# RWKV stage of a two-block layer kernel: the elementwise part of the next head group moved beside the inverse, and output products moved between steps of the last scan

## The reference

```python
r, k, v, wl, al, gl = jnp.split(feat, splits, axis=-1)
w = -jax.nn.softplus(-(w0 + jnp.tanh(wl) @ w2)) - 0.5
a = jax.nn.sigmoid(a0 + al @ a2)
g = jax.nn.sigmoid(gl) @ g2
kk = heads(k * k_k)
kk = kk * lax.rsqrt(jnp.sum(kk * kk, axis=-1, keepdims=True) + 1e-12)
k = k * (1.0 + (a - 1.0) * k_a)
...
def step(state, inp):
    r_t, k_t, v_t, kk_t, b_t, d_t = inp
    sa = jnp.einsum('bhvk,bhk->bhv', state, -kk_t)
    state = (state * d_t[:, :, None, :] + sa[..., None] * b_t[:, :, None, :]
             + v_t[..., None] * k_t[:, :, None, :])
    return state, jnp.einsum('bhvk,bhk->bhv', state, r_t)
...
x = x + jnp.concatenate([mla_out, rw_out], axis=-1) @ w_o
x = x + hier_moe(rms_norm(x, g_ffn), ...)
```

## Time and profile before

| | us |
|---|---|
| median of 3 runs (2466.19 to 2469.96) | 2467.66 |
| the profiled execution's own time | 2463.41 |
| its span in the trace | 2461.6 |
| RWKV stage, first product of `rows` 0 to `rw_out` 4 | 263.1 to 531.6 |
| output products and router | 531.6 to 566 |

### The profile page before, as it was taken

How to read it: one execution, slowest core, us unless ns; L and a number is a source line. 1 busy time by engine, 2 the same in 40 slices (tenths; PEclk the granted TensorE clock), 3 DMA queues, 4 the chain that set the end, 5 groups by cost and what they waited for, 6 DMA issues and landing times.

```text
span 2461.6 us, 30787 instructions
## 1 busy us (share of the span) xinstructions
PE 2324.6 (94%) x12524; PEld 1654.6 (67%) x12524; DVE 1233.2 (50%) x2169; ACT 746.1 (30%) x1172; POOL 646.4 (26%) x288
## 2 busy tenths in 40 slices
PE   8989787797999989999999999999999999999999
PEld 3334455544444467668878888888766887888887
DVE  4455555533556531774355767310187445577610
ACT  3333222212111143443233333223354223333311
POOL 0000000002000033224444444444313444444443
PEclk9999888878999999999999999999999999999999
DMA  5521000035999932113333333222211333333322
GB/s 220 135 71 35 15 2 2 2 134 196 373 409 409 356 114 88 60 52 95 94 94 95 98 99 94 93 96 98 86 52 61 94 95 93 96 101 94 95 80 99
DMA packets 80258, 287.79 MB, mean 117 GB/s; under 512 B 9299, under 2 KB 10323, under 8 KB 79478
## 3 DMA queue, kind: packets, MB, share of 16 engines
q1 hardware_dynamic: 76726, 279.56, 33.1%
q0 software_dynamic: 1408, 4.20, 0.5%
q10 hardware_dynamic: 1984, 2.06, 0.2%
HBM read 278.11 MB, written 16.07 MB: 120 GB/s over the span
## 4 chain that ended last, share of the span: by engine, by line
PE 80%; DVE 9%; DMA 5%; issue 3%; ACT 2%; POOL 1%; ACTq 0%; SPq 0%; DVEq 0%; another core or an unknown queue 0%; POOLq 0%
PE bank L1899 12%; PE bank L1901 12%; PE bank L1900 12%; PE bank L529 5%; DMA arena<-in_stream 4%; PE bank L2048 3%; PE bank L2049 3%; PE bank L2047 3%; DVE arena L392 3%; PE bank L1513 2%; PE bank L855 2%; PE bank L1884 2%; PE bank L1886 2%; PE bank L1885 2%; PE bank L1481 2%
## 5 line engine op out<-in xcount | busy, mean ns | idle before, releaser
L1634 POOL TENSOR_TENSOR ring_low<-ring,W_high 128x1024 fp32r<-128x1024 f32 x252 | 606.2, 2406 | 1124.5 <-ACT W_high L402 1124.5
L1899 PE MATMUL bank<-H_high,W_high 128*128 128x512 f32 x1408 | 555.5, 395 | 7.9 <-ACT arena L402 5.9
L1901 PE MATMUL bank<-H_high,ring_low 128*128 128x512 f32 x1408 | 548.5, 390 | 0.0
L1900 PE MATMUL bank<-H_low,W_high 128*128 128x512 f32 x1408 | 548.1, 389 | 0.0
L402 ACT ACTIVATE W_high<-ring 128x1024 fp32r<-128x1024 f32 x264 | 279.8, 1060 | 872.2 <-PE bank L1901 552.6
L1899 PEld LDWEIGHTS bank<-H_high,W_high 128*128 128x128 f32 x1408 | 264.3, 188 | 77.9 <-issue 23.2
L1901 PEld LDWEIGHTS bank<-H_high,ring_low 128*128 128x128 f32 x1408 | 264.3, 188 | 55.9
L1900 PEld LDWEIGHTS bank<-H_low,W_high 128*128 128x128 f32 x1408 | 264.4, 188 | 55.7 <-issue 1.9
L392 DVE TENSOR_TENSOR arena<-bank,root 128x512 f32<-128x512 f32 x116 | 79.7, 688 | 309.9 <-PE bank L1901 309.7
L402 ACT ACTIVATE arena<-bank 128x512 f32<-128x512 f32 (+5 forms) x175 | 74.6, 438 | 315.2 <-PE bank L830 115.9
L398 DVE SCALAR_TENSOR_TENSOR arena<-arena 128x512 f32<-128x512 f32 (+3 forms) x63 | 117.8, 1870 | 99.1 <-ACT arena L406 98.5
(11 more groups left out here) (264 smaller groups left out, 3239.2 us busy)
## 6 DMA issues: line engine op xcount, KB each, us to landing
ring<-in_stream SPq DMA_DIRECT2D x289, 512.0 KB, 3.6
arena<-in_stream SPq DMA_DIRECT2D x31, 2048.0 KB, 12.9
arena<-in_stream SPq DMA_DIRECT2D x31, 1024.0 KB, 10.2
sorted_x<-in_zero_row SPq DMA_DIRECT2D x4, 2048.0 KB
arena<-sorted_x SPq DMA_DIRECT2D x15, 512.0 KB, 16.3
X<-in_x SPq DMA_DIRECT2D x2, 1024.0 KB, 7.9
ring<-in_stream SPq DMA_DIRECT2D x1, 2048.0 KB, 7.9
out<-X SPq DMA_DIRECT2D x8, 256.0 KB, 7.0
```

The costliest lines, as they stand in the source:

```text
L1634: return G.tensor_tensor(ring_low[:, slot, :], ring[:, slot, :], W_high[:, s % 2, :].bitcast(F32), ALU.subtract)
L1899: mm(ps[:, :], wh[:, k, :], H_high[:, k, :], start=k == 0, stop=False)
L1900: mm(ps[:, :], wh[:, k, :], H_low[:, k, :], start=False, stop=False)
L1901: i = mm(ps[:, :], wl[:, k, :], H_high[:, k, :], start=False, stop=k == KD - 1)
```

## The change

It has three parts.

1. `rwkv_prepare` is split into `rwkv_early` (`feed`, `rows`, `roots`, `root`, `bonus`, `turned`: the elementwise part, with `rows` and `root` each cut so that the products stand ahead of VectorE's part) and `rwkv_invert` (from `blocks` on). In round c = 0 to 3 the inverse of group c stands beside the scan of group c - 1 and the early part of group c + 1. The products `rg` and the turned `v` move to the end, in `turned`.
2. MT, TT, TKA, XX and MK move to the place of the attention's weights `uq`, which are no longer needed. DVE's wait for `rta` goes. The lower halves m are placed by `HALVES_AT`: three in the opening, then 3 and 4 in round 0, 5 in round 1, 6 and 7 in round 2.
3. For column tiles 0 to 6, contraction tile 4 of the upper half stands between `step` n and `state` n of the last scan, and tiles 5 and 6 behind `state` n, into a bank of their own (`wq{n}`), which DVE adds to X. After the scan only tile 7 is left for them; m = 7 keeps all four.

```diff
+def rwkv_invert(c):
+
+    yield "blocks", c, 0
+    yield "keyed", c, 0
     for lev in LEVELS:
         yield "cross", c, lev
         yield "grow", c, lev
...
-BESIDE = "pss" * 4 + "ps" * 10 + "pspp"
+def rwkv_early(c):
+
+    for part in ("feed", "rows", "roots", "root", "bonus", "turned"):
+        yield part, c, 0
+
+
+EARLY_OUT = 7
+HALVES_AT = {("feed", 0): [0], ("roots", 0): [1], ("bonus", 0): [2], ("feed", 1): [3], ("bonus", 1): [4], ("bonus", 2): [5], ("feed", 3): [6], ("bonus", 3): [7]}
+BESIDE = "iss" * 4 + "e" + "iss" + "e" + "iss" * 2 + "e" + "iss" + "is" + "e" + "is" * 2 + "e" + "ii" + "e"
...
+    for part in rwkv_early(0):
+        yield from with_halves(part)
+    for c in range(4):
+        invert, scan, early = rwkv_invert(c), rwkv_scan(c - 1) if c else iter(()), rwkv_early(c + 1) if c < 3 else iter(())
         for who in BESIDE:
...
+    for part, c, n in rwkv_scan(3):
+        yield part, c, n
+        if part in ("step", "state") and n < EARLY_OUT:
+            yield f"out_{part}", c, n
...
-        W.update(YB=W["LW"], MT=W["LW"], TT=W["A"], TKA=W["KK"], KH=W["KK"], KT=W["KP"], BT=W["B"], XX=W["SQ"], MK=W["RS"],
+        W.update(YB=W["LW"], KH=W["KK"], KT=W["KP"], BT=W["B"],
                  BH=W["ENL"], AT=W["ELX"])
+        for i, n in enumerate(("MT", "TT", "TKA", "XX", "MK")):
+            W[n] = par(w1, W1, "uq", 512 * i, 512)
...
-                for k in range(4, KD):
+                first = KD - 1 if m < EARLY_OUT else 4
+                for k in range(first, KD):
...
+            if part == "half":
+                latent_half(pe, n, range(4))
+            elif part == "out_step":
+                pe.e.wait_ge(*pe.emptied(f"wq{n}"))
+                pe.e.wait_ge(*pe.nth("rw_out", 3))
+                mm(bank_of(f"wq{n}")[:, :], out_weights(pe, n)[:, 4, :], H[:, 4, :], start=True, stop=False)
+            elif part == "out_state":
+                w = out_weights(pe, n)
+                mm(bank_of(f"wq{n}")[:, :], w[:, 5, :], H[:, 5, :], start=False, stop=False)
+                mm(bank_of(f"wq{n}")[:, :], w[:, 6, :], H[:, 6, :], start=False, stop=True).then_inc(pe.fills(f"wq{n}"), 1)
...
-            if part == "rows":
-                if c:
-                    dv.e.wait_ge(*dv.filled(f"rta{c - 1}_1"))
+            if part == "half":
+                add_latent_half(dv, n)
+            elif part == "out_state":
+                dv.e.wait_ge(*dv.filled(f"wq{n}"))
+                if n == 0:
+                    dv.e.wait_ge(*dv.taken("wp7"))
+                tt(X[:, n, :], X[:, n, :], bank_of(f"wq{n}")[:, :], ALU.add).then_inc(dv.takes(f"wq{n}"), 1)
```

More of the change, by code:

```diff
@@ L710, in rwkv_pe @@
             e, q = pe.e, c % 2
-            if part == "rows":
+            if part == "half":
[8 more added lines that the diff above has]
+                mm(bank_of(f"wq{n}")[:, :], w[:, 6, :], H[:, 6, :], start=False, stop=True).then_inc(pe.fills(f"wq{n}"), 1)
+            elif part == "feed":
                 pe.e.wait_ge(*pe.emptied(f"ru{c}"))
@@ L719, in rwkv_pe @@
                 mm(bank_of(f"ra{c}")[:, :], w2a2[64:128, cw], RAW[64:128, 12, 1:513], start=True, stop=True).then_inc(pe.fills(f"ra{c}"), 1)
+            elif part == "roots":
+                pe.e.wait_ge(*pe.emptied(f"rkk{c}"))
+                pe.e.wait_ge(*pe.nth("kksq", c + 1))
+                mm(bank_of(f"rkk{c}")[:, :], cc("blk64"), W["SQ"], start=True, stop=True).then_inc(pe.fills(f"rkk{c}"), 1)
+            elif part == "bonus":
+                pe.e.wait_ge(*pe.emptied(f"rb{c}"))
+                pe.e.wait_ge(*pe.nth("rkr", c + 1))
+                mm(bank_of(f"rb{c}")[:, :], cc("blk64"), W["YB"], start=True, stop=True).then_inc(pe.fills(f"rb{c}"), 1)
+            elif part == "turned":
+                pe.e.wait_ge(*pe.nth("hats", c + 1))
+                for x, src in (("b", W["BH"]), ("k", W["KH"]), ("a", W["AT"]), ("v", RAW[:, 8 + c, 1:513])):
+                    turn_feature(pe, c, x, src)
                 pe.e.wait_ge(*pe.emptied(f"rg{c}"))
@@ L723, in rwkv_pe @@
                 mm(bank_of(f"rg{c}")[:, :], par(w1, W1, "g2", c * P, P), RAW[:, 13, 1:513], start=True, stop=True).then_inc(pe.fills(f"rg{c}"), 1)
[L724 to L739, removed]
             elif part == "blocks":
@@ L986, in rwkv_act @@
             q = c % 2
-            if part == "rows":
+            if part == "feed":
                 if c == 0:
@@ L996, in rwkv_act @@
                 act_(W["A"], bank_of(f"ra{c}")[:, :], ACT.Tanh, bias=small[:, 12 + c:13 + c], scale=0.5).then_inc(sc.takes(f"ra{c}"), 1)
[L997 to L1001, removed]
-                act_(W[f"TKV{q}"], bank_of(f"rt{c}_v")[:, :], ACT.Copy).then_inc(sc.takes(f"rt{c}_v"), 1)
-            elif part == "root":
+            elif part == "roots":
                 log_exp_tables()
@@ L1014, in rwkv_act @@
             elif part == "turned":
-                for x, d in (("b", f"TKB{q}"), ("k", f"TKK{q}"), ("a", "TKA")):
+                for x, d in (("b", f"TKB{q}"), ("k", f"TKK{q}"), ("a", "TKA"), ("v", f"TKV{q}")):
                     sc.e.wait_ge(*sc.filled(f"rt{c}_{x}"))
                     act_(W[d], bank_of(f"rt{c}_{x}")[:, :], ACT.Copy).then_inc(sc.takes(f"rt{c}_{x}"), 1)
+                sc.e.wait_ge(*sc.filled(f"rg{c}"))
+                if c >= 2:
+                    sc.e.wait_ge(*sc.nth("rw_out", c - 1))
+                act_(W[f"G{q}"], bank_of(f"rg{c}")[:, :], ACT.Copy).then_inc(sc.takes(f"rg{c}"), 1)
             elif part == "keyed":
```

31 lines of the change are left out of this document (15 added, 16 removed).

## The result

The change made the kernel a little slower: 2472.6 us (median of 17 runs, 2467.5 to 2473.9) against 2465.9 (17 runs on the same chip), a ratio of 1.0021 with an interval of 1.0015 to 1.0028. I had forecast 2459 and given slower 0.15; it lies just inside my range of 2446 to 2473, on the wrong side of the kernel before. The profiled execution took 2472.6 us, its span is 2470.8, 9.2 more than before.

The account below looks back on a forecast made before the run. Rounds were taken as PE-DVE chains with no engine full. Opening and rounds gain 6.7 us, scan and output 1.8: -8.5 on the profiled 2463.4 gives 2454.9, plus 4.3 to the median: 2459, range 2446 to 2473.

Parts of the forecast that it names:

- the clock term: Rounds 0 to 2: half clock behind each `rows` and `root` wait, 5 us counted, 2.1 on the path, 11 in all.
- my 233.4: Opening and all rounds up to the last scan: 222.4 at full clock plus 11 of clock, against 240.1 before.
- The bricks: Stage and step lengths read from the earlier trace, such as 30.8 us for a round's inverse half, added up for the new order.
- The stalls: PE waiting for DVE's `rows` and `root` in rounds 0 to 2: 3.4 and 4.3 us each.
- The first pass: Round 0, inverse 0 beside early part 1 and lower halves 3 and 4: 46 us before the clock's cost.
- The second step in a level: A second scan step between `cross` and `grow` of an inverse level shows as 2.4 us, at best 0.3.
- The last scan: Three output products join each step; PE bounds it at 4.2 us instead of 2.4: 12.6 more, plus 1.6 of clock.
- rival 3: The last scan stays at half clock, a step takes 7.5 us, the kernel is slower at 2482; chance 0.14.
- The output: Column tiles 1 to 6 lose three products each, 16.2 us, less 2.3 for a half-clock start: 13.9 saved.
- tile 7's weights: Output stage: they land at 13.9 us after `rw_out` 4, PE needs them at 14.6, fitting by little.
- 1 (full clock): The clock stays full in the rounds: -23.4 us in all, 2444; chance 0.15.
- Rival 2: Each `rows` and `root` delays the chain by its whole length, 1.4 us more six times: 2467.5, no change; chance 0.23.

Follow-up runs that it names:

- part 3 alone: The kernel before with only the output products placed between the steps of the last scan, rounds untouched: 2469.15 us, ratio 1.0012.
- the shifted order: The changed kernel with `state` n - 1 right ahead of `step` n instead of right behind `step` n - 1: 2468.51 us, ratio 1.0012.
- the shifted order with the halves in the stalls: The changed kernel with `state` n - 1 right ahead of `step` n and lower output halves moved over `rows` and `root`: 2453.54 us, ratio 0.9946.

## Why the prediction was wrong

- **The step that failed** is the clock term: "Six times, and nearly always: 11 us", for "two stalls of 3.4 and 4.3 us in each of rounds 0 to 2". There are three pauses in rounds 1 and 2 and one in round 3, since DVE's masks of `blocks` hold PE up for 1.7 and 1.1 us. And the third costs 5.3 us by the rows from `keyed` to `feed`, where I had 1.8 for each. Covering it with idle products took 13.8 us off the kernel and made the three rounds 14.6 us shorter in all; the opening and the rounds came out 13.3 above my 233.4. The kernel before waits in `blocks` too, but once and not twice, and its clock held there in rounds 1 and 2; I took the 30.8 us of that half of the round as a brick, and the clock that was in it with it.
- **The length of a stretch at half clock** was mis-sized too. I counted 5 us behind each stall, and had read the earlier trace rows as one pause with its half clock up to 336. The trace before has two, a wait of 3.42 us up to 318.0 and one of 4.86 up to 327.8, with full clock between them:

```profile
320.00:322.00 2.00, 2.00 (x4) 0.81 (x3) 0.58 (x1) 1.95 (x5) 0.00 (x0) 0.50 0.00 0
323.00:325.00 2.00, 0.00 (x0) 0.00 (x0) 1.97 (x4) 0.00 (x0) 0.00 (x0) 1.00 0.00 0
```

Behind the first the clock was at half for 3 us, behind the second for 10. In the changed kernel it was 6 and 3 us behind the two stalls of round 0, and 10 and 7 in rounds 1 and 2: 43 in all where I had 30.
- **The bricks added up, in part by luck.** Where that pause is covered by idle products and nothing else is changed, rounds 1 to 3 take 60.1, 62.9 and 39.5 us. I had 56 and 59.6, with 3.7 of clock on each, and 41: 59.7, 63.3 and 41. But the second step was too dear (below), and it hid that the stalls' half clock lasted 17 and 13 us in these two rounds and not 10. That this kernel ran at 2458.8 us, where I had forecast 2459 for the changed one, is luck as well: its stages are 0.8 us shorter than my 292.2 (300.7 less 8.5), the parts ahead of and behind them 4.1 us longer than before, and the 4.3 that I had added from the profiled execution to the median are 2.5 by the 17 runs.
- **The stalls** of `rows` and `root` are 3.25 and 3.82 us in round 0, and 4.0 and 3.7 in rounds 1 and 2, forecast 3.4 and 4.3, with DVE as releaser and half clock behind each.
- **The first pass** took 49.2 us, forecast 46 and 3.7 of clock.
- **The second step in a level** I took at 2.4 us. That is the step of the earlier trace rows, which runs at half clock, in a sum that was to hold at full clock. In round 3 of the changed kernel, at full clock and with no elementwise part beside it, the levels with two steps follow each other every 5.90 us (L854 begins a `state`; the other one of the level stands between these two, at 488.02), against 4.34 with one:

```profile
485.58 0.33 PE L854 MATMUL bank<-arena 64*64 64x64 f32 x4
...
491.48 0.33 PE L854 MATMUL bank<-arena 64*64 64x64 f32 x4
```

So the second step costs 1.6 us, and four of them in a round were too dear by some 3 us, which hid in part what I had left out.
- **The last scan**: the clock rose to 1.00, as I read it from the earlier trace rows, and rival 3, by which it stays at half, fell. The Trainium skill, "TensorE: Matmul & The Clock Gate", section "HAM oscillation — how this bites in real kernels", advises to keep a tile's contraction products together, for a kernel whose products wait for DMA in between. Such waits the last scan doesn't have, and in this trace the products taken apart brought the clock up. PE waits for nothing there once the steps have begun, so it bounds the step, as I had it. The term was mis-sized: a step is 4.55 us and not 4.2, 2.4 in all, since its own pieces take 1.85 beside three products of 0.9 and not 1.5; the stage took 43.5 us, forecast 40.5.
- **The output** took 21.0 us, forecast 20.5, and tile 7's weights were just in time.
- **The rivals**: 1 (full clock) and 3 fell. Rival 2, 2467.5, comes nearest of them to 2472.6, but by the wrong mechanism: its stalls together are no longer than I had them.

## What to carry to other kernels

When an order is woven anew, list every place where TensorE runs out of work, short ones of 2 us too, and give each its own stretch at half clock, read from the windows of 1 us around it. One length for all doesn't do: behind the stalls it was 3 to 10 us here, behind the two pauses in `blocks` 13 to 14, and behind the stall of `root`, with `bonus` and a lower half following each time, 3 us in round 0 and 7 in rounds 1 and 2. Work that can stand anywhere, like the lower halves, belongs into those pauses; moving it there was worth 28 us, four times what the whole change lost. And read a stage's length together with its granted clock before it becomes a brick, for a length measured at full clock holds only for as long as the new order keeps it.

## What the runs showed of the hardware

- Adding work in a pause can save time: nine idle products, 8.5 us of PE work, took 13.8 us off in the pause, and put 11 on elsewhere.
- A higher granted clock is no gain by itself: the last scan, with three products more in each of seven steps, went from 0.52 to 0.99 with part 3 alone, and the kernel was 3 us slower.
- Behind the same wait of 1.6 to 1.7 us in `blocks` the clock held (two rounds of the kernel before, and round 1 with the shifted order), was at half for 3 to 4 us (part 3 alone) or for 10 (the shifted order with the halves in the stalls).
- PE listed as busy says little about such a stretch: between 340 and 350 us of the changed kernel each window of 2 us has 2.00 of busy time, at clock 0.50, and the work from `keyed` to `feed` takes 13.95 us so and 8.6 at full clock.
